# One merged stage between the AB projection and its out-projection, and two weight slots filled earlier

## The reference

```
qa,ka,va,ga,qb,kb,vb,gb,lr_f,lr_b = split(z @ w_in)
qa, ka = rope(qa), rope(ka)                    # image tokens only
la = log_sigmoid(lr @ w_lr + b_lr) / 16        # forward and backward
oa = retention, both directions (4 heads, fixed decay)
ob = gated linear attention (GLA), both directions, chunks of 64
ya = head_norm(oa, centred) * gn_a ;  yb = head_norm(ob) * gn_b
y  = concat(silu(ga) * ya, silu(gb) * yb) @ w_out
```

## Time and profile before

| | us |
|---|---|
| median of 3 runs | 3023.14 (3021.97 to 3024.15) |
| the profiled execution | 3028.02 |
| its span, on which the trace's clock runs | 3026.2 |
| TensorE busy in it | 2434.4 (80%) |
| VectorE busy | 655.3 (22%) |
| ScalarE busy | 368.0 (12%) |
| GpSimd busy | 121.1 (4%) |
| the part between the AB projection and its out-projection | 316.7 to 514.6 |

### The profile page before, as it was taken

One profiled execution on the slowest core, in us unless ns is written; L12 is line 12 of the kernel. 1 busy time (PEld: TensorE's weight loads), 2 busy tenths in 40 slices (PEclk: granted clock), 3 DMA queues, 4 the chain that ended last, 5 costly groups with the idle time before them and its releaser, 6 DMA issues. The chain is left out here.

```text
span 3026.2 us, 35279 instructions
## 1 busy us (share of the span) xinstructions
PE 2434.4 (80%) x14539; PEld 1323.5 (44%) x14539; DVE 655.3 (22%) x1418; ACT 368.0 (12%) x647; POOL 121.1 (4%) x166
## 2 busy tenths in 40 slices
PE   7999665899888883994668888884737999785998
PEld 3333443444343432332443333332424777563776
DVE  2000235631000004102752200003153100253000
ACT  0000121211111111000411101011013000210000
POOL 0000001000000001000010000001010000000000
PEclk9999866899999996997979999997879999897999
DMA  7787600199999995675039999995221344422442
GB/s 272 296 302 289 210 12 23 71 417 422 423 422 423 422 421 213 239 264 203 7 142 421 423 423 423 423 422 227 95 75 63 117 153 152 143 70 70 152 152 78
DMA packets 180355, 724.54 MB, mean 239 GB/s; under 512 B 14469, under 2 KB 72709, under 8 KB 114480
## 3 DMA queue, kind: packets, MB, share of 16 engines
q1 hardware_dynamic: 165824, 676.24, 57.5%
q0 software_dynamic: 8656, 25.83, 2.7%
q10 hardware_dynamic: 5792, 21.32, 1.8%
HBM read 699.04 MB, written 23.25 MB: 239 GB/s over the span
## 5 line engine op out<-in xcount | busy, mean ns | idle before, releaser
L1770 PE MATMUL bank<-ring,arena 128*64 128x512 f32 x1632 | 380.4, 616 | 71.5 <-DMA ring<-moe_w_up 47.1
L433 PE MATMUL bank<-ring,actT 128*128 128x512 f32 x768 | 347.0, 605 | 4.8 <-DMA ring<-c_w_qkv 2.4
L2145 PE MATMUL bank<-actT,ring 128*128 128x256 f32 x1408 | 307.3, 379 | 2.2 <-PEq L517 2.2
L2145 PEld LDWEIGHTS bank<-actT,ring 128*128 128x128 f32 x1408 | 267.4, 190 | 46.9 <-issue 11.6
L1400 PE MATMUL bank<-arena 128*64 128x512 f32 x1088 | 241.2, 595 | 27.0 <-ACT arena L1468 23.3
L1770 PEld LDWEIGHTS bank<-ring,arena 128*64 128x64 f32 x1632 | 116.2, 141 | 330.2 <-issue 217.2
L433 PEld LDWEIGHTS bank<-ring,actT 128*128 128x128 f32 x768 | 143.6, 192 | 207.8 <-issue 207.8
L549 PE MATMUL bank<-misc,arena 128*128 128x128 f32 (+1 forms) x278 | 52.8, 370 | 175.7 <-PEq L1976 53.5
L1759 PEld LDWEIGHTS bank<-arena 128*128 128x128 bf16 x5280 | 160.8, 99 | 34.2 <-issue 29.3
L1759 PE MATMUL bank<-arena 128*128 128x64 bf16 x5280 | 165.2, 195 | 5.9 <-DVE arena L1500 4.3
L1508 DVE TENSOR_TENSOR arena<-arena,bank 128x512 f32<-128x512 f32 x34 | 23.4, 688 | 663.3 <-ACT arena L1466 663.3
(11 more groups left out here) (343 smaller groups left out, 1957.3 us busy)
## 6 DMA issues: line engine op xcount, KB each, us to landing
ring<-moe_w_gate SPq DMA_DIRECT2D x136, 1024.0 KB, 24.0
arena<-moe_w_down SPq DMA_DIRECT2D x136, 1024.0 KB, 21.6
ring<-ada_w SPq DMA_DIRECT2D x96, 1024.0 KB, 7.1
ring<-moe_w_up SPq DMA_DIRECT2D x68, 1024.0 KB, 23.9
actT<-moe_w_up SPq DMA_DIRECT2D x68, 1024.0 KB, 24.7
ring<-ffn_w SPq DMA_DIRECT2D x66, 1024.0 KB, 5.2
made_scratch<-arena ACTq DMA_DIRECT2D x34, 512.0 KB, 7.8
ring<-ab_w_in SPq DMA_DIRECT2D x14, 1024.0 KB, 8.2
```

The costliest lines, as they stand in the source:

```text
L433: mm = nc.tensor.matmul(self.bank[g % 6][:, :], lhsT(m, k), halves[k // 4][:, k % 4, :], start=(k == 0), stop=(k == KT - 1))
L1770: return self.nc.tensor.matmul(self.bank[j // 2][64 * i:64 * i + 64, :], xs[:, S * kt:S * kt + S], piece[:, k * DE:(k + 1) * DE], start=(k ...
L2145: mm = nc.tensor.matmul(bank[2 * (j % 2) + which][:, f * SEQ:(f + 1) * SEQ], w[:, k, f * P:(f + 1) * P], self.actT[:, k * T:k * T + SEQ], ...
```

## The change

Steps 2 to 8 above become one stage. Its engines' lists are written out by hand, and every dependence has a semaphore of its own (31 new ones, `ab_...`). In detail:

- The tables and parameters of steps 2, 4 and 5 are loaded by GpSimd at the start of the AB projection's stage, into `mod` (k_ret, k_rope_a, gate weights and biases) and the arena (k_gla). The gains `gn` are loaded in the merged stage, once the low-rank projection is done.
- `mod` is therefore taken until the last mask is applied. The load of layer 0's modulation vectors moves from SyncE at the start of step 2 to ScalarE's queue behind `masked 4`, between the second and third exponential of pair 0. That of layer 1 moves into the first stage of `moe` (layer 0), and `rows_for_c` waits for it.
- Context tiles are turned first, image tiles when rotated. Scores and mixes of the heads interleave with the gates, the cumulative sums of pair 0 with the last mix. The sums of pair 1 go between the attention blocks and the combine of pair 0, all but the fifth, which comes behind that combine.
- The head norms: retention blocks are normed during pair 1, blocks of pair 0 after their copy, and those of pair 1 per tile, straight from PSUM without a copy, in the tile order 0, 2, 1, 3. Silu and the gains are applied to the gates beforehand. Four small powers on GpSimd take the place of the last ones of one large.
- The final transposes follow tile by tile, and ScalarE alone evicts them.
- In `moe`, both layers, SyncE loads pieces R+2 and R+3 of the first pair at the start of the first stage; the expert loop's start loads the other four.

The core of the diff (the lists of TensorE, VectorE and ScalarE; helper bodies left out where they are those of before):

```diff
+        def tables(pool):
+            nc.gpsimd.memset(wlr, 0.0).then_inc(self.pool_done.up(), 1)
+            pool.wait_ge(self.pool_done.sem, self.pool_done.at(1))
+            self.load_params(pool, [
+                (mod[:, ROPE:ROPE + 512].rearrange("p (t n) -> p t n", t=2), I["k_rope_a"].rearrange("(t p) n -> p t n", p=P)),
...
+                (A(GT, 1152), I["k_gla"]), (mod[:, 0:4096], I["k_ret"])])
...
+                turn_o(0, 2, 0, 0)
...
+                pe.wait_ge(self.params_in.sem, tables_in)
+                pe.wait_ge(*at("lr_taken", 1))
+                for t in range(4):
...
+                    nc.tensor.matmul(bank[4 + t][:, :], self.arena[0:32, LRT + t * P:LRT + (t + 1) * P], wlr, start=True,
+                                     stop=True).then_inc(*up("gate_made"))
+                for n in range(4):
+                    pe.wait_ge(*at("roped", n // 2 + 1))
+                    pe.wait_ge(*at("o_taken", n + 1))
+                    turn_o(4 + n, n // 2, n % 2, n)
+                pe.wait_ge(*at("o_taken", 8))
+                score(0)
+                pe.wait_ge(*at("gate_taken", 4))
+                score(1)
+                mix(0)
+                score(2)
+                mix(1)
+                pe.wait_ge(*at("masked", 2))
+                score(3)
+                mix(2)
+                pe.wait_ge(*at("la_ready", 1))
+                for b in range(3):
+                    sums(0, b)
+                mix(3)
+                for b in (3, 4):
+                    sums(0, b)
+                turn_keys(0)
+                make_states(0)
+                make_att(0)
+                for b in range(4):
+                    pe.wait_ge(*at("att_ready", b + 1))
+                    sums(1, b)
+                pe.wait_ge(*at("chain_done", 1))
+                for h in range(2):
+                    for t in range(4):
+                        mm = combine(0, h, t, bank[4 + h][:, t * P:(t + 1) * P])
+                    mm.then_inc(*up("c_made"))
+                sums(1, 4)
+                turn_keys(1)
+                make_states(1)
+                make_att(1)
...
+                pe.wait_ge(*at("chain_done", 2))
+                for t in last:
+                    for h in range(2):
+                        mm = combine(1, h, t, combined(t, h))
+                    mm.then_inc(*up("c_made"))
+                for n, t in enumerate(last):
+                    pe.wait_ge(*at("tile_ready", n + 1))
+                    for g in range(2):
+                        for q in range(4):
+                            mm = nc.tensor.transpose(bank[2 * n + g][:, q * P:(q + 1) * P], group(t, 4 * g + q), self.ident)
...
             @block.sync
             def _(sp):
-                self.load_mod(sp, 0, 2, 6, (0, 1))
-                self.load_mod(sp, 1, 0, 2, (0, 1))
                 self.feed(sp)
...
+                for h in range(2):
+                    take_mix(h)
+                nc.scalar.activation(A(G, 4096), A(G, 4096), ACT.Silu).then_inc(*up("g_ready"))
+                take_mix(2)
+                exps(0, 0)
+                exps(0, 1)
+                take_mix(3)
+                act.wait_ge(*at("masked", 4))
+                self.load_mod(act, 0, 2, 6, (0, 1))
+                for n in range(2, 6):
+                    exps(0, n)
+                borders(0)
+                take_keys(0)
+                for n in range(5):
+                    exps(1, n)
+                for h in range(2):
+                    act.wait_ge(*at("c_made", h + 1))
...
+                exps(1, 5)
...
+                mask(2)
+                mask(3)
+                apply_decay(0)
+                dve.wait_ge(*at("mix_done", 4))
+                V_.memset(actT[:, ATT[0]:ATT[0] + 1024], 0.0)
...
+                for t in range(4):
+                    ins = V_.tensor_tensor(A(G + t * D, D), A(G + t * D, D), actT[:, GN:GN + D], ALU.mult)
+                link(ins)
+                link(V_.memset(actT[:, ATT[1]:ATT[1] + 1024], 0.0))
+                take_att(0)
+                chain(0)
...
+                gather_stats(part_a, group)
...
+                apply_decay(1)
+                for t, j in part_a:
+                    ins = V_.scalar_tensor_tensor(group(t, j), group(t, j), moment(t, j, 1), gate(t, j), ALU.subtract, ALU.mult)
...
+                take_att(1)
+                chain(1)
...
+                tail_stats(0)
...
+                for n in range(4):
+                    if n < 3:
+                        tail_stats(n + 1)
+                    tail(n)
```

In `moe`, in `experts` and in `rows_for_c`:

```diff
             @block.sync
             def _(sp):
+                if layer == 0:
+                    self.load_mod(sp, 1, 0, 2, (0, 1))
+                first_pair = self.pair_sources(layer, 0)
+                for n in range(2):
+                    src, k, _ = first_pair[R + 2 + n]
+                    sp.dma_start(A(OVW + n * SLOT, SLOT).rearrange("p (k n) -> p k n", k=k), src).then_inc(self.spare_in[layer][2 + n], 16)
                 self.feed(sp)
...
-                for m in range(R, 2 * R):
+                for m in (R, R + 1, R + 4, R + 5):
                     load_main(m, first[m])
...
+        self.mod_here(dve)
```

More of the change, by code:

```diff
@@ L455, in _ @@
                                        self.xres[0:64, t * D:(t + 1) * D]).then_inc(sm["x_unmixed"].up(16), 16)
+                if tables is not None:
+                    tables(pool)
                 for n, (l, r) in enumerate(rounds):
@@ new lines, in mixer_ab @@
+        self.st_linear_hosting(lambda m, k: actT[:, k * T + m * P:k * T + m * P + P], AB_CHUNKS, dest, AB_ROUNDS, tables=tables)
+        tables_in = self.params_in.total
+        states = lambda p, d, c: (actT, mod)[p][:, (d * 8 + c) * P:(d * 8 + c + 1) * P]
+        decay = lambda p, d, c: self.cols[:, 32 + 16 * p + 8 * d + c:33 + 16 * p + 8 * d + c]
+        att = lambda p, t, h: actT[:, ATT[p] + t * 256 + h * P:ATT[p] + t * 256 + (h + 1) * P]
+        order = [[4, 5, 6, 7, 0, 1, 2, 3], [7, 6, 5, 4, 3, 2, 1, 0]]
@@ L799, in _ @@
+                exps(1, 5)
+                borders(1)
+                take_keys(1)
+                for n, t in enumerate(last):
+                    for g in range(2):
+                        act.wait_ge(*at("tile_turned", 2 * n + g + 1))
+                        nc.scalar.activation(self.put_for_mixed(t, g), dims(bank[2 * n + g][:, :], [P, 4], [1, P]),
+                                             ACT.Copy)
             @block.vector
@@ new lines, in chain @@
+                def chain(p):
+                    dve.wait_ge(*at("state_made", p + 1))
+                    for n in range(1, 8):
+                        for d in range(2):
+                            c = order[d][n - 1]
+                            add = bank[4 + 2 * d + c % 2][:, (c // 2) * P:(c // 2 + 1) * P]
+                            if n == 1:
+                                ins = V_.tensor_copy(states(p, d, order[d][1]), add)
+                            else:
+                                ins = V_.scalar_tensor_tensor(states(p, d, order[d][n]), states(p, d, c), decay(p, d, c), add, ALU.mult, ALU.add)
+                        if n < 7:
+                            link(ins)
+                    ins.then_inc(*up("chain_done"))
@@ new lines, in gather_stats, with about_zero @@
+                def gather_stats(pairs, source):
+                    for t, j in pairs:
+                        ins = V_.bn_stats(sums6(t, j), source(t, j))
+                    link(ins)
+                    for t, j in pairs:
+                        ins = V_.bn_aggr(moment(t, j, 2), sums6(t, j))
+                    link(ins)
+                def about_zero(first, free, free2):
+                    out, mean, var = dims(stat[:, first:], *free), dims(stat[:, 64 + 2 * first:], *free2), dims(stat[:, 65 + 2 * first:], *free2)
+                    link(V_.tensor_tensor(out, mean, mean, ALU.mult))
+                    V_.scalar_tensor_tensor(out, out, LN_EPS, var, ALU.add, ALU.add).then_inc(*up("power_in"))
```

488 lines of the change are left out of this document (230 added, 258 removed).

## The result

The changed kernel takes **2940.07 us** (median of 4 runs, 2935.2 to 2944.24) against 3023.22 of the kernel before on the same chip (4 runs, 3021.97 to 3024.15): ratio 0.9725, 95% interval 0.9707 to 0.9742. The forecast was 2942. The profiled execution took 2944.24, span 2942.4, so 83.8 less than the one before.

A forecast was written before the change was run, and what follows sets the result against it. Bound: between AB projection and out-projection, a chain of short steps with no engine full. Merged stage 77 us less, slots 4.5 less, next stage 0.5 more: 81 less, from the median 3023.14 to 2942 us; range 2927 to 2961.

The forecast's parts named there:

- c: Merged stage, three sums, last mix, two ScalarE issues (1.1 us), then exponentials and decays (3.7 us): ends at 368.0 us.
- f: Merged stage, end of first combine to second: sum, states, attention at 6.51, copy and chain, 19.0 us; retention scaling fits beside.
- h: Merged stage's end: four tiles' transposes 5.57 us, copy 0.6, stage edge 0.4, plus 1.7 for handovers; ends at 438.
- main term: The merged stage: out-projection starts at 438 instead of 514.6 us, 77 us less.
- Step i: 3.3 MB of tables moved into the projection stage: costs nothing, or 7.8 us if the cover were gone.
- Step j: Two early slots in the expert loops: layer 0 gains 0.5 us, layer 1 gains 4; together 4.5 less.
- Step k: Stage after the merged one: parameters delayed 7.2 us against 6.6 slack; costs 0.5 us in all, at most 2.5 per layer.
- Fast combines: Rival, GLA combines: both run at clock 1.00 in half the time, 14.3 us less, 2928; chance 0.14.
- Slow middle: Rival, retention part of the merged stage: runs at 1.2 GHz, 19.6 us more, 2962, half of it 2952; chance 0.11.
- Collision: Rival, next stage: parameters 7 us late stop TensorE 2.5 us per layer, handovers cost 5 more, 2951; chance 0.13.
- Phases in series: Rival, merged stage: VectorE serves phases one after the other, only waits for tables and edges go, 2982; chance 0.03.
- slower than before: Rival, after the merged stage: TensorE stays at 1.2 GHz through out-projection and first expert pair, costing 83 us, 3025; chance 0.02.

The follow-up runs named there:

- run 1: Changed kernel with the two early slots loaded at the expert loop's start again, as before the change: 2934.11 us, ratio 0.971.
- run 2: Changed kernel with SyncE waiting for the parameters before its loads, and VectorE no longer waiting for layer 1's modulation vectors: 2931.84 us, ratio 0.9704.
- run 10: The changed kernel measured again, with no edit: 2939.34 us, ratio 0.9725.
- run 6: Changed kernel with the retention half's head norms put behind pair 1's whole chain of states: 2941.44 us, ratio 0.9728.
- run 7: Changed kernel with the seven tables loaded at the merged stage's start, all waited for at once: 2947.1 us, ratio 0.9747.
- run 5: Changed kernel with scaling of the retention half's first part put ahead of pair 1's last decay on VectorE: 2939.75 us, ratio 0.9723.
- run 8: Changed kernel with pair 1's fourth cumulative sum computed five times over, to fill TensorE's wait: 2933.74 us, ratio 0.9703.
- run 3: Changed kernel with each combine's two heads issued in turn, on opposite halves, attention blocks ahead together: 2931.66 us, ratio 0.9693.
- run 11: Changed kernel with parameters before slots, heads in turn, sums before the last mix, and scaling in VectorE's wait: 2926.12 us, ratio 0.9682.
- run 12: run 11 with the scaling put back behind pair 1's last decay: 2919.53 us, ratio 0.9662.
- run 9: Changed kernel with one whole-column matmul per direction replacing two pieces in the combines, leaving out half the states: 2942.86 us, ratio 0.9735.

## Why the prediction was right, step by step

| step | forecast | measured in the profiled execution |
|---|---|---|
| a) low-rank to first scores | 19.3 | 19.1 |
| b) scores and mixes | 19.6 | 18.6 |
| c) sums, exponentials, to the last keys | 12.4 | 10.1 |
| d) to the first combine | 14.1 | 14.2 |
| e) first combine | 14.3 | 14.0 |
| f) to the second combine | 19.0 | 17.6 |
| g) second combine | 14.3 | 14.2 |
| h) transposes and edge | 8.3 | 6.0 |
| low-rank to out-projection | 121.3 | 113.9 |

**The main term, 77 of 81, was read from the right place** and came out at 84. That total is the difference of two stretches of one execution each. In three other executions with this merged stage unchanged (runs 1, 2 and 10) the stretch was 109.2 to 109.4, so the term would have been about 88.5 there and the miss 11.5. No run undoes the merge as a whole: runs 6 and 7 take back the place of the norms (4.7) and of the tables (10), and the rest of the 84 rests on the steps of the table, which the trace shows one by one. Most terms lean long. In c the last keys are turned 2.3 us sooner than I had it; I had priced the two issues on ScalarE rightly (1.1 forecast, 1.14 measured), but the exponentials overlap them more than I allowed. In f the attention took 3.50, not 6.51: the row I took it from was made at a low clock, and I did not ask which clock the new order would give it. Half of that gain was lost again to the scaling, of which the forecast said that it fits between the decay and the first attention block; run 5 shows 1.8 us of it on the path. In h the allowance of 1.7 for handovers was not needed. Slips of the working are under 1 us each: the copy of 0.6 in a is added as 0.9; the parts of d add up to 374.8, not 375.2; and its states are priced at 2.0 where the row shows 2.60 and the new order took 3.11.

**Step i**, the tables at nothing in the projection: the start of the merged part is at the same time (316.45 against 316.73; 315.7 to 320.0 in the other traces, so a cost of a few us would not be seen), and run 7 gives the worth of the move as 10 us.

**Step j**, the slots: 4.0 forecast and 3.4 measured in layer 1; 0.5 forecast in layer 0 and nothing measured (527.0 against 526.2 before, 526.7 in run 1), which is too close to tell. The DMA gap of 3 us is there as foretold.

**Step k failed in size**: 0.5 forecast, 2.7 measured in layer 0 up to the expert loop (4.7 at the first normed tile's transposes; 0 in layer 1). The mechanism had been named, with 2.5 per layer as its far end; what was wrong is the slack. I measured the parameters' delay against the first normed tile, 27.7 us into the stage. What they have to meet is the end of TensorE's first tile, 14.0 us in. They had been in time by 5.8 us, not 6.6, and they came 8.7 later, not 7.2: 16.8 us in. TensorE stopped for 2.78. The other 1.7 of the second tile is the low clock that the kernel before met in its third. In layer 1 the parameters came 12.1 us in (VectorE's first step at 1457.23, out-projection from 1445.11), inside the 14.0, and it cost nothing. In run 10 the stop was 1.57, the loss at the transposes 1.9 and up to the expert loop 1.1. Run 1, which leaves the 2 MB of slots out of this stage, shows them as the cause of the stop, and run 2 shows that it is enough to issue them, with the modulation vectors, behind the parameters. The rule of the Trainium skill that was weighed there (DMA: Bandwidth & Descriptors, "Queues, rings and completion order": the engines take turns between queue rows) gave 0; the measurement decides, and it is a stop of 2.78.

The errors had opposite signs: the merged stretch brought 7.0 us more than forecast, the slots brought 1.9 less (2.6 in both layers together, for 4.5), and the next stage cost 2.2 more. That the forecast of 2942 came within 2 us of the median is in part luck, since the errors offset each other and since the course that the clock took in an execution is worth 4.5 us by itself.

**The rivals.** *Fast combines* was half right. It did not happen in the profiled execution, but the first combine ran at 1.00 in runs 1, 2, 7, 8 and 10. Where the merged stage was unchanged (1, 2, 10) that brought 4.5 us of the stretch and not 7, since the attention ahead of it was slow instead. *Slow middle*: no, 2.84 a mix. *Collision*: its parameter part happened, in one layer of the two; its handovers did not. *Phases in series* and *slower than before*: no; the out-projection's first 32 records took 13.97, the fast rate.

## What to carry to other kernels

When stages are merged, price each step at the clock that its new neighbours give it, and find for every load that moves the first instruction that really waits for it. On a path of short steps, small matmuls that use different rows of the array belong next to each other: here such an order took a stretch of 109 to 114 us down to 100, and 8 us off the median. A gap in one engine's list is filled safely only if no other edit shortens it; the scaling in the wait took 1.8 us off the way between the combines alone, and cost 6 beside the faster combine.

## What the runs showed of the hardware

- A granted clock of 0.50 can last through 14 us of uninterrupted matmuls: 7.50 of 7.50 us busy at 0.50 in the first combine. With the two heads' pieces side by side it rose within 3.3 to 6 us of the same step (runs 3, 11 and 12); with whole-column matmuls from one half of the rows it did not rise in 14.9 (run 9).
- Pieces of 64x64 in the two halves of the rows overlap at either clock: 16 records take 1.13 us at 0.50 and 0.67 at 1.00, where 8 of one half take 1.13 and 0.66 (runs 3 and 10, and the changed kernel).
- One program took either of two courses through the same stage: a low clock that begins just ahead of the states of pair 0 lasts 3.4 us and another one comes at the combine, or it lasts 13.9 us and the combine is fast; 113.9 or 109.4 us in all. What decides between them was not found.
- The out-projection of layer 0 met some 3.5 us at a granted clock of 0.50 in 11 of 14 traces, in its second, third or fourth tile, with a stop ahead of it or without (the kernel before, runs 11 and 12).
- With 3 MB on SyncE's queue, issued at the same time, the 1.2 MB of parameters on GpSimd's let VectorE go on 16.8 us after the stage's start (15.6 to 16.8 in the traces with this order); with no load of SyncE's beside them (run 2), 8.1.
